# A norm's gain and shift moved to the eviction of its transposes, with three waits of the RWKV products made finer

## What is computed

```
h = layer_norm(ALPHA * h + relu(h @ w1)**2 @ w2, ln2_g, ln2_b)
xx = token_shift(h) - h
xr, xw, xk, xv, xa, xg = (h + xx * mu[i] for i in range(6))
r, k, v = xr @ w_rkv[0], xk @ w_rkv[1], xv @ w_rkv[2]
w_log = -softplus(-(w0 + tanh(xw @ w1) @ w2)) - 0.5
a = sigmoid(a0 + (xa @ a1) @ a2)
g = sigmoid(xg @ g1) @ g2
...                      # the delta rule over 512 tokens, its norm, times g, @ w_o
h = layer_norm(ALPHA * h + that, ...)
```

## Time and profile before

| | us |
|---|---|
| median of 3 runs (lowest, highest) | 1346.65 (1345.14, 1346.79) |
| the profiled execution | 1351.93 |
| its span | 1350.2 |
| PE busy in the span | 1299.2 (96%) |
| DVE busy | 685.1 (51%) |
| POOL busy | 578.8 (43%) |
| ACT busy | 508.1 (38%) |

### The profile page before, as it was taken

One profiled execution on the slowest core, in us unless ns is written; L12 is line 12 of the kernel. 1 busy time (PEld: TensorE's weight loads), 2 busy tenths in 40 slices (PEclk: granted clock), 3 DMA queues, 4 the chain that ended last, 5 costly groups with the idle time before them and its releaser, 6 DMA issues.

```text
span 1350.2 us, 23124 instructions
## 1 busy us (share of the span) xinstructions
PE 1299.2 (96%) x9233; PEld 1069.6 (79%) x9233; DVE 685.1 (51%) x909; ACT 508.1 (38%) x878; POOL 578.8 (43%) x356
## 2 busy tenths in 40 slices
PE   7999999999999998999989999999999999999996
PEld 6888788888888884487767888888888888888885
DVE  2486831112344468646468788866661111344447
ACT  4363232232322323324344677755232222322230
POOL 4344344444544451225444455636054444444440
PEclk9999999999999998999999999987999999999999
DMA  7233243332644321464433112103344333333311
GB/s 267 78 96 123 62 141 93 94 100 70 173 120 119 101 79 47 162 218 150 160 126 106 34 56 74 34 18 110 95 116 116 94 93 95 105 96 93 93 62 63
DMA packets 113580, 139.54 MB, mean 103 GB/s; under 512 B 10416, under 2 KB 86240, under 8 KB 113504
## 3 DMA queue, kind: packets, MB, share of 16 engines
q1 hardware_dynamic: 108896, 121.67, 30.0%
q10 hardware_dynamic: 4608, 16.78, 3.3%
HBM read 123.76 MB, written 14.68 MB: 103 GB/s over the span
## 4 chain that ended last, share of the span: by engine, by line
PE 82%; DVE 13%; ACT 2%; issue 2%; DMA 0%; SPq 0%; ACTq 0%; DVEq 0%
PE bank L1702 37%; PE bank L1797 9%; PE bank L1798 9%; PE bank L1799 9%; PE bank L2008 2%; DVE a_lo L1174 2%; DVE x_tok L1204 2%; DVE x_tok L1206 2%; DVE stats L1193 2%; PE bank L1892 2%; DVE x_tok L1226 1%; PE bank L2056 1%; PE bank L2109 1%; PE bank L2179 1%; PE bank L2106 1%
## 5 line engine op out<-in xcount | busy, mean ns | idle before, releaser
L483 POOL TENSOR_TENSOR w_lo<-raw,w_hi 128x1024 fp32r<-128x1024 f32 x176 | 432.4, 2462 | 614.4 <-ACT w_hi L684 564.7
L684 ACT ACTIVATE w_hi<-raw 128x1024 fp32r<-128x1024 f32 x176 | 184.2, 1056 | 282.8 <-PE bank L1702 275.8
L1702 PE MATMUL bank<-w_hi,a_hi 128*128 128x512 f32 x756 | 235.6, 393 | 9.3 <-DVE a_lo L1174 9.3
L1797 PE MATMUL bank<-xT_hi,w_hi 128*128 128x512 f32 (+1 forms) x640 | 236.3, 369 | 3.9 <-POOL w_lo L483 3.9
L1798 PE MATMUL bank<-xT_lo,w_hi 128*128 128x512 f32 (+1 forms) x640 | 235.4, 368 | 0.0
L1799 PE MATMUL bank<-xT_hi,w_lo 128*128 128x512 f32 (+1 forms) x640 | 235.4, 368 | 0.0
L1702 PE MATMUL bank<-w_lo,a_hi 128*128 128x512 f32 x756 | 234.7, 392 | 0.0
L1702 PE MATMUL bank<-w_hi,a_lo 128*128 128x512 f32 x756 | 233.8, 390 | 0.0
L1174 DVE TENSOR_TENSOR a_lo<-big,a_hi 128x512 fp32r<-128x512 f32 x64 | 141.3, 2213 | 178.7 <-ACT a_hi L703 175.6
L1291 DVE TENSOR_TENSOR big<-relu 128x512 f32 (+1 forms) x64 | 45.8, 716 | 274.0 <-ACT relu L809 274.0
L1702 PEld LDWEIGHTS bank<-w_hi,a_hi 128*128 128x128 f32 x756 | 140.9, 188 | 43.5 <-issue 15.0
(11 more groups left out here) (304 smaller groups left out, 1659.3 us busy)
## 6 DMA issues: line engine op xcount, KB each, us to landing
raw<-in_ffn_w SPq DMA_DIRECT2D x128, 512.0 KB, 4.0
raw<-in_rw_w_rkv SPq DMA_DIRECT2D x24, 512.0 KB, 3.6
raw<-in_gm_w_in SPq DMA_DIRECT2D x16, 512.0 KB, 4.4
early<-proj SPq DMA_DIRECT2D x8, 1024.0 KB, 6.1
proj<-stage ACTq DMA_DIRECT2D x14, 512.0 KB, 3.0
proj<-low_stage ACTq DMA_DIRECT2D x10, 512.0 KB, 5.7
raw<-in_gm_w_out SPq DMA_DIRECT2D x8, 512.0 KB, 3.6
raw<-in_rw_w_o SPq DMA_DIRECT2D x8, 512.0 KB, 3.5
```

The source lines that it names most:

```text
L483: nc.gpsimd.tensor_tensor(w_lo[:, j, :], raw[:, j, :], w_hi[:, j, :].bitcast(F32), ALU.subtract).then_inc(w_lo_ready, 1)
L684: nc.scalar.activation(w_hi[:, j, :], raw[:, j, :], ACT.Copy).then_inc(w_hi_ready, 1)
L1702: last = nc.tensor.matmul(bank[2 * t + h][:], a[:, j, tok], w[:, h * HALF:(h + 1) * HALF], start=start and m == 0, stop=stop and m == 2)
L1797: nc.tensor.matmul(dst, w_hi[:, j, col], xT_hi[:, k, tokens], start=k == 0, stop=False)
```

## The change

Five things change.

- The norm of "down0" is cut in two. DVE (`residual_stats`) only subtracts the mean and multiplies by the reciprocal of the deviation, half by half, with semaphore z_ready. PE transposes this z. Gain and shift, which lie along the partitions after a transpose, are applied at the eviction: by ACT (`turned_scaled`) for all halves but the last, by DVE for the last, in pieces of 128 columns, one for each k. ACT's order becomes std 0, std 1, tile 0, std 2, tile 1, std 3, tile 2, first half of tile 3.
- For this ln2_g and ln2_b are loaded as 16 more rows beside mu, by two more DMAs, and transposed with it.
- The residual gets its gain and shift later (`scale_residual`): 8 operations on 128x1024 on DVE, one after each slab of receptance. The loads of gn, which overwrite the gains, move behind it, in front of the loads of early. xxT's first four slabs now wait for the last half of xT too.
- In `project_g` the matmuls of the 32 remaining rows come first, each bank is then closed by its three matmuls and signalled by itself. DVE copies the first four banks ahead of its work for key's first two slabs. ACT evicts wa 1 ahead of the stores of g.
- In value's last group PE waits for each slab when tile 0 comes to it.

The semaphores x_half and g_projected are counted anew to match. The diff, cut to its core:

```diff
...
-mu = sb("mu", [P, 6, KT])
-mu_rows = sb("mu_rows", [6 * KT, P])
+mu = sb("mu", [P, 8, KT])
+mu_rows = sb("mu_rows", [8 * KT, P])
+GAIN, SHIFT = 6, 7
...
                     if (name, i, j) == ("rw_out", 0, 1):
 
+                        sp.wait_ge(x_ready, 2 * TT)
+                        for g, vector in enumerate((rw_gn_g, rw_gn_b)):
+                            sp.dma_start(gn[:, g, :], vector.partition_broadcast(P).rearrange("p a n -> p (a n)")
+                                         ).then_inc(gn_in, 16)
...
-                    sp.dma_start(mu_rows[:], rw_mu[0].rearrange("m (k p) -> (m k) p", p=P)).then_inc(mu_in, 16)
+                    sp.dma_start(mu_rows[0:6 * KT, :], rw_mu[0].rearrange("m (k p) -> (m k) p", p=P)).then_inc(mu_in, 16)
+                    for m, vector in ((GAIN, ln2_g), (SHIFT, ln2_b)):
+                        sp.dma_start(mu_rows[m * KT:(m + 1) * KT, :], vector[0].rearrange("(k p) -> k p", p=P)
+                                     ).then_inc(mu_in, 16)
...
-                    sp.wait_ge(x_ready, 2 * TT)
-                    for g, vector in enumerate((rw_gn_g, rw_gn_b)):
-                        sp.dma_start(gn[:, g, :], vector.partition_broadcast(P).rearrange("p a n -> p (a n)")
-                                     ).then_inc(gn_in, 16)
...
-            sp.wait_ge(x_half, len(normed))
+            sp.wait_ge(x_half, len(normed) - 1)
...
+    def turned_scaled(t):
+
+        for h in range(1 if t == TT - 1 else 2):
+            act.wait_ge(x_turned, 2 * 2 * TT + 2 * t + h + 1)
+            for k in range(4):
+                last = nc.scalar.activation(xT[:, 4 * h + k, PAD + t * P:PAD + (t + 1) * P],
+                                            bank[2 * t + h][:, k * P:(k + 1) * P], ACT.Identity,
+                                            bias=mu[:, SHIFT, 4 * h + k:4 * h + k + 1],
+                                            scale=mu[:, GAIN, 4 * h + k:4 * h + k + 1])
+            last.then_inc(xT_ready, 1)
...
-            nc.scalar.activation(mu[:].rearrange("p m k -> p (m k)"), bank[5][:, 0:6 * KT], ACT.Copy
+            nc.scalar.activation(mu[:].rearrange("p m k -> p (m k)"), bank[5][:, 0:8 * KT], ACT.Copy
...
-    finish_norm("down0", FT, 2, 2)
+    for t in range(TT):
+        if t >= 2:
+            turned_scaled(t - 2)
+        std_of(2, t)
+    turned_scaled(2)
+    turned_scaled(3)
...
     drain_wa(0)
+    drain_wa(1)
     store_g(0)
-    drain_wa(1)
     store_g(1)
     drain_wa(2)
     drain_wa(3)
...
+    def residual_stats(name, which):
+
+
+        product = row_products.index(name)
+        dve.wait_ge(gains_in, 32 * (which + 2))
+        for t in range(TT):
+            for h in range(2):
+                if (t, h) == (0, 0):
+                    dve.wait_ge(tile_summed, product * (TT - 1) + 1)
+                elif h == 0:
+                    dve.wait_ge(half_summed, normed.index(name) * (TT - 1) + t)
+                elif t < TT - 1:
+                    dve.wait_ge(tile_summed, product * (TT - 1) + t + 1)
+                else:
+                    dve.wait_ge(slab_used, first_slab[name] + COUNT[name])
+                y = x_tok[:, t, h * HALF:(h + 1) * HALF]
+                then(nc.vector.scalar_tensor_tensor(y, y, ALPHA, bank[2 * t + h][:], ALU.mult, ALU.add))
+                last = done.inc(nc.vector.bn_stats(stats[:, h, :], y))
+            dve.wait_ge(dve_done, last)
+            then(nc.vector.bn_aggr(mean_var[:], stats[:].rearrange("p h s -> p (h s)")))
+            nc.vector.tensor_scalar(mean_var[:, 1:2], mean_var[:, 1:2], LN_EPS, None, ALU.add
+                                    ).then_inc(var_ready, 1)
+            dve.wait_ge(std_ready, (which + 1) * TT + t + 1)
+            then(nc.vector.reciprocal(rstd[:], std[:]))
+            for h in range(2):
+                y = x_tok[:, t, h * HALF:(h + 1) * HALF]
+                nc.vector.tensor_scalar(y, y, mean_var[:, 0:1], rstd[:, 0:1], ALU.subtract, ALU.mult
+                                        ).then_inc(z_ready, 1)
+        t = TT - 1
+        dve.wait_ge(x_turned, 2 * 2 * TT + 2 * TT)
+        for k in range(4):
+            last = nc.vector.tensor_scalar(xT[:, 4 + k, PAD + t * P:PAD + (t + 1) * P],
+                                           bank[2 * t + 1][:, k * P:(k + 1) * P], mu[:, GAIN, 4 + k:4 + k + 1],
+                                           mu[:, SHIFT, 4 + k:4 + k + 1], ALU.mult, ALU.add)
+        last.then_inc(xT_ready, 1)
+
+    def scale_residual(m):
+        t = m // 2
+        dve.wait_ge(x_turned, 3 * 2 * TT)
+        if m % 2 == 0:
+            dve.wait_ge(z_ready, 2 * t + 2)
+            done.inc(nc.vector.tensor_tensor(x_tok[:, t, :], x_tok[:, t, :], gains[:, 0, :], ALU.mult))
+        else:
+            dve.wait_ge(dve_done, done.n)
+            nc.vector.tensor_tensor(x_tok[:, t, :], x_tok[:, t, :], gains[:, 1, :], ALU.add).then_inc(x_ready, 1)
...
-    residual_norm("down0", 1, 2, False)
-
-
     dve.wait_ge(mu_ready, 1)
+    residual_stats("down0", 1)
+
...
-        dve.wait_ge(xT_ready, 3 * 2 * TT - (1 if k < KT // 2 else 0))
+        dve.wait_ge(xT_ready, 3 * 2 * TT)
...
-            dve.wait_ge(g_projected, t + 1)
+            dve.wait_ge(g_projected, 2 * t + h + 1)
...
+        if u == 0:
+            drain_g(0)
+            drain_g(1)
...
             low_of(k // SLOTS, k % SLOTS, m0, lambda k: mix[:, k % SLOTS, :])
             if k + 2 < KT:
                 mix_slab(k + 2)
-            if u == 0 and k < 2:
-                drain_g(k)
+            if u == 1:
+                scale_residual(k)
             if u == 0 and k == 1:
                 drain_g(2)
                 drain_g(3)
...
         if order is not None:
-            for j in range(SLOTS):
-                arrived(count // SLOTS - 1, j)
             for t, j in order:
+                if t == 0:
+                    arrived(count // SLOTS - 1, j)
                 last = row_tile(j, t, False, j == SLOTS - 1)
...
     def turn_x(norms, t):
         for h in range(2):
-            if norms is not None and (t, h) == (TT - 1, 0):
-                pe.wait_ge(x_half, norms + 1)
+            if norms == 1:
+                pe.wait_ge(z_ready, 2 * t + h + 1)
+            elif norms is not None and (t, h) == (TT - 1, 0):
+                pe.wait_ge(x_half, norms if norms else 1)
             elif norms is not None:
                 pe.wait_ge(x_ready, norms * TT + t + 1)
...
-            pe.wait_ge(mu_in, 16)
-            nc.tensor.transpose(bank[5][:, 0:6 * KT], mu_rows[:], ident[0:6 * KT, 0:6 * KT]).then_inc(mu_turned, 1)
+            pe.wait_ge(mu_in, 48)
+            nc.tensor.transpose(bank[5][:, 0:8 * KT], mu_rows[:], ident[0:8 * KT, 0:8 * KT]).then_inc(mu_turned, 1)
...
-            pe.wait_ge(low_split, 5)
+            pe.wait_ge(low_split, 4)
         else:
             pe.wait_ge(proj_read, 8)
         for b in range(COPIES):
             tok, col = slice((t + b // 2) * P, (t + b // 2 + 1) * P), slice(b % 2 * HALF, (b % 2 + 1) * HALF)
-            for m, (a, w) in enumerate(((low_g_hi, lg2_hi), (low_g_hi, lg2_lo), (low_g_lo, lg2_hi))):
-                nc.tensor.matmul(bank[G_BANK[t] + b][:], a[:, tok], w[:, col], start=m == 0, stop=False)
+            rows = slice(b * REST, (b + 1) * REST)
+            nc.tensor.matmul(bank[G_BANK[t] + b][:], low_gb[rows, tok], lg2b[rows, col], start=True, stop=False)
         for b in range(COPIES):
             tok, col = slice((t + b // 2) * P, (t + b // 2 + 1) * P), slice(b % 2 * HALF, (b % 2 + 1) * HALF)
-            rows = slice(b * REST, (b + 1) * REST)
-            last = nc.tensor.matmul(bank[G_BANK[t] + b][:], low_gb[rows, tok], lg2b[rows, col], start=False, stop=True)
-            if b % 2:
-                last.then_inc(g_projected, 1)
+            for m, (a, w) in enumerate(((low_g_hi, lg2_hi), (low_g_hi, lg2_lo), (low_g_lo, lg2_hi))):
+                if (t, b, m) == (0, 0, 2):
+                    pe.wait_ge(low_split, 5)
+                last = nc.tensor.matmul(bank[G_BANK[t] + b][:], a[:, tok], w[:, col], start=False, stop=m == 2)
+            last.then_inc(g_projected, 1)
...
```

More of the change, by code:

```diff
@@ L281, in trunk @@
         x_turned, xT_ready, xT_split = sem("x_turned"), sem("xT_ready"), sem("xT_split")
+        z_ready = sem("z_ready")
         var_ready, std_ready, x_ready, v_ready = sem("var_ready"), sem("std_ready"), sem("x_ready"), sem("v_ready")
```

## The result

The changed kernel takes 1353.51 us (median of 20 executions, 1346.98 to 1360.39), the kernel before, measured with it, 1346.64 (20, 1344.98 to 1354.87). The ratio of all executions is 1.0042 [1.0025, 1.0059], slower by 0.4%; between the two medians lie 6.9 us. The forecast was 1345.4, with a range of 1340.5 to 1348.8. The profiled execution took 1355.93, with a span of 1354.2, against 1351.93 and 1350.2 before.

A forecast was written before the change was run, and what follows sets the result against it. PE was taken to bound the kernel, with 82% of the chain of waits, so edits pay only where PE stands still. 0.7 + 2.26 + 4.65 - 6.4 = 1.2 gained, median 1346.65 to 1345.4, range 1340.5 to 1348.8.

The forecast's parts named there:

- Low-rank g (B): Low-rank projections: earlier DVE copies of g remove PE's whole wait, 2.26 gained, bounds 1.5 to 2.5.
- Value (D): Value's last group: PE's idle and the half clock behind it go, decay sums start 4.65 earlier, bounds 3.9 to 5.2.
- Rival 4: Value edit does nothing, as ACT's order or a late early load holds the decay sums: 1348 to 1350, chance 0.07.
- The norm (A): First down projection's norm: xxT starts 0.7 earlier, behind ACT's 12 pieces at pitch 0.375; bounds 2.4 gained to 0.5 lost.
- the errata table: Skill's ScalarE table for the norm's evictions: 0.25 us per piece, by which the norm's gain would be 1.9, not 0.7.
- The residual's gains (C): Receptance: eight new DVE operations delay a_lo at two places, 6.4 lost, bounds 3.0 to 8.8.
- The first place: Receptance's slab 1: a_lo comes late behind the first scale operation and a POOL subtraction; PE stands about 3.4.
- The second place: Receptance between a_lo(4) and a_lo(7): three scale operations delay a_lo, 3.0 lost; one meets POOL's subtraction.
- rival 3: Receptance's stalls of about 3.2 pull PE's clock down, 1.7 each: 1347.1 or 1348.8, chance 0.13.
- Rivals 1 and 2: Receptance: 1, smaller loss, 1343.2 or 1342.0, chance 0.30; 2, more scale operations meet a subtraction, 2.4 each, chance 0.08.

The follow-up runs named there:

- g_only: Kernel before with only the low-rank g edits (matmul order, signal per bank, earlier copies, drain order): 1344.31 against 1346.88, ratio 0.9985.
- value_only: Kernel before with only the value edit (each slab of the last group waited for when tile 0 comes to it): 1345.69, ratio 0.9997; again 1343.19, ratio 0.9977.
- scale_in_tail: Changed kernel with the residual's eight operations in one DVE block ahead of receptance's first a_lo: 1339.31 against 1346.88, ratio 0.9951.
- stalls_filled: Changed kernel with 24 matmuls on zeros ahead of each of two PE waits in receptance: 1351.47 against 1347.35, ratio 1.0026.
- norm_only: Changed kernel without the value edit and the low-rank g edits, residual operations still in receptance: 1355.99 against 1346.88, ratio 1.0051.
- first_place: Changed kernel with residual operations 0 to 3 left in receptance and 4 to 7 in a block ahead of value: 1348.51 against 1347.35, ratio 0.9995.

## Why the prediction was wrong

**Low-rank g (B)** was right: 2.26 forecast, 2.7 in the trace, 2.4 over all traces, 2.6 in the median of `g_only`. What stood behind the moved copies cost nothing.

**Value (D)** was right where it acts: 4.65 forecast, 4.7 measured, and the same 30.3 from value's start in the changed kernel, `value_only` and `scale_in_tail` (686.98 less 656.64). Rival 4 is out. The forecast carried it to the end unchanged: in the medians of the edit alone only 1.2 to 3.9 of it arrive.

**The norm (A)** went as described, ACT's pieces ending last, and was undersized: 0.7 forecast, 1.2 measured. The pitch was 0.35 instead of 0.375. The Trainium skill (ScalarE: Activation LUTs, What ACT_TABLE_LOAD costs) gives 186 ns plus 0.833 per element, 93 for each pointer operand and 93 of overlap: an estimate of 0.386 for a piece, with which the measured 0.35 roughly agrees. It has the term for the pointer that the errata table lacked and that I had taken from the rows. My figure of 1.9 for A by the errata table doesn't follow from my own sum either: twelve pieces at 0.25 instead of 0.375 are 1.5 less, which makes 2.2.

**The residual's gains (C)** is the step that failed. I had 3.4 + 3.0 = 6.4; it was 10.7. The first place went as forecast, 3.10 against 3.4: the first scale operation stood behind POOL's subtraction (3.42) and the a_lo behind the next (2.83). The second place failed in one sentence: "POOL's subtraction, which a_lo(7) met, is met by scale(5) instead". DVE's operations there run without a gap, and POOL, which comes in the middle, gets its turn only behind the last of the residual's. The idle moved from a_lo (0.77) to w_lo (3.40), together 3.9 over the 0.25 of before. So the stalls grew by 7.0. The upper bound of 8.8 holds them; it had one more hand-over of 2.4 in it, while it was POOL that starved.

Of the rest of C 3.4 is rival 3 (the remaining 0.3 I can't place): the stalls pull the clock down, 1.7 each. It had a chance of 0.13 and two places; both happened, and `stalls_filled` shows that this is its own term. I argued against it that 2.26 idle in the low-rank part did not do it. But the forecast stalls were 3.4 and 3.0, between that row and the 4.26 that did, and every stall of 3.1 or more in receptance did it in all traces, and one of 2.95 in `norm_only` as well. The range did take in rival 3, with both stalls, at 1348.8. It left out two errors on the same side.

**What no step had** is more half clock outside the stages that the change touches. Locally the change loses 2.1 (1.2 + 2.7 + 4.7 - 10.7); the medians say 6.9. So the errors of the four steps explain 3.3 of the 8.1 by which the forecast missed, and 4.8 are left. With the local loss of 2.1 alone the time would have come out near 1348.7, just inside the range: what put it outside is this term.

The mean clocks of the executions bear it out as a term of the clock. Of the 10.8 us more at half clock, the two stalls in receptance make 6.8, and the fall that value no longer has takes 3.4 off; 7.4 are left, worth 3.7, and they lie elsewhere. The other 1.1 of the 4.8 is what the medians differ by more than the means. The changed kernel's trace has 10.2 more behind the delta rule. In how many of its executions that is so can't be read off, as its 20 times spread evenly from 1347.0 to 1360.4, and why the clock stays low longer is open. The sum of the parts' medians stays short of the 6.9: 1.5 and 2.6 gained, 1.2 to 3.9 gained by value, 10.4 lost, is 2.4 to 5.1 lost.

Rivals 1 and 2 are out: receptance cost more, but not by more scale operations that meet a subtraction.

## What to carry to other kernels

Work that is nobody's bottleneck must be placed by the gaps of the queue it joins, not by its share of busy time: the same eight operations cost 10.7 us one after each slab, and nothing in a block at the end of the product before, where DVE was idle. Where two engines exclude each other, ask for both directions: who stands behind a long operation, and who gets no turn while the other runs without a gap. A stall of PE near 3 us is to be priced with its clock, about half as much again here. And where executions of one kernel differ by their clock, compare the time at half clock too: 5.4 of the loss here stood there, and only 0.4 in waits.

## What the runs showed of the hardware

- DVE's two-tensor operations back to back can keep a GpSimd subtraction waiting over several operations that were issued after it: 7.38 and 7.43 instead of 2.40 in three kernels. In the Trainium skill (GPSIMD Engine Reference, Specifications) GpSimd's SBUF interfaces are shared with VectorE and contended, which these rows bear out; that section doesn't say who wins. In `norm_only` the turn went to POOL at the same offset within 0.01 us (2.81), and in the first place it got its turns between DVE's operations, so neither the order of issue nor a missing gap alone decides, and what does stays open.
- Whether a stall pulled PE's clock down went by its length: in receptance, value and the low-rank part 2.26 left it at 1.00, and 2.95, 3.10, 3.40 and 4.26 came with 3.4 us at 0.50 (6.8 once, in `norm_only`). The fall came between 0.9 us before PE resumed (`norm_only`, 623.4 against 624.31) and 1.5 after (`first_place`, 622.0 against 620.56). The falls in the delta rule and behind it have no such stall in front.
- The late low stretch has two lengths, 13.7 and 23.9, and nothing between them in 13 traces. It is the longer one where the clock fell 1.0 or more behind the matmul after the last wait of 1.01, the shorter one where it fell by 0.7.
- A tensor_scalar of 128x512 float32 with two operands per partition, in SBUF, takes 0.50 (two in a row take 1.00), where the same shape with two tensors takes 0.69.
